# Attention stages in groups of two: three transposed banks per group, one of them copied out by ScalarE

## The reference

```
def nsa_mixer(h, ...):                      # 16 heads of 64, 4 groups of keys and values
    q, kc, vc, ks, vs, kw, vw, gates = split(h @ w_in)
    k_cmp, v_cmp = compress(kc), compress(vc)        # gelu(blocks @ w1 + b1) @ w2, 15 blocks
    p_c = masked_softmax(q k_cmp * scale + bias)     # compressed branch
    o_cmp = p_c @ v_cmp
    o_sel = softmax(q ks * scale + bias) @ vs        # 256 tokens: all 4 blocks are selected
    o_win = softmax(q kw * scale + bias) @ vw        # the window covers all 256 tokens
    g = sigmoid(gates)
    return (g[0] * o_cmp + g[1] * o_sel + g[2] * o_win) @ w_out

def fox_mixer(h, w_in, b_f, w_out):
    q, k, v, f = split(h @ w_in)
    cum = cumsum(log_sigmoid(f + b_f))
    p = masked_softmax(q k * scale + cum_i - cum_j)
    return (p @ v) @ w_out

for i in range(2):
    h = h + 0.5 * norm(swiglu(norm(h)))
    h = h + norm(mixer_i(norm(h)))
    h = h + 0.5 * norm(swiglu(norm(h)))
```

## Time and profile before

| | |
|---|---|
| time before, median of 3 runs | 1019.35 us (1019.15 to 1019.61) |
| the profiled execution, its own time | 1017.23 us |
| its span in the trace | 1015.4 us |
| TensorE busy in the span | 1003.4 us (99%) |
| VectorE / ScalarE / GpSimd busy | 637.9 / 518.0 / 118.8 us |
| NSA, 237 to 338 us of the span, FoX, 742 to 823 us | the two stretches that the change touches |

### The profile page before, as it was taken

The page is one execution under the profiler, slowest core; times in us unless marked ns, Lnnn a source line. Parts: engine busy times, 40 slices in busy tenths (PEclk is TensorE's granted clock), DMA queues, the critical chain, the costliest instruction groups (busy, mean ns, idle before and its releaser), DMA issues.

```text
span 1015.4 us, 13811 instructions
## 1 busy us (share of the span) xinstructions
PE 1003.4 (99%) x5701; PEld 849.7 (84%) x5701; DVE 637.9 (63%) x761; ACT 518.0 (51%) x711; POOL 118.8 (12%) x214
## 2 busy tenths in 40 slices
PE   8999999999999999999999999999999999999997
PEld 7888888897767898888889888888888789888886
DVE  5656555756686765555576655557568776555654
ACT  5544544644564555444465444445456665454442
POOL 1000000213263300000030000001103320000000
PEclk9999999999999999999999999999999999999999
DMA  9767779268303365566825565692485345655651
GB/s 269 257 199 259 234 258 299 86 187 248 126 2 126 125 207 186 188 201 213 291 83 194 182 205 177 196 316 98 139 281 179 108 145 176 197 195 179 206 175 74
DMA packets 138422, 189.55 MB, mean 187 GB/s; under 512 B 7442, under 2 KB 120439, under 8 KB 138360
## 3 DMA queue, kind: packets, MB, share of 16 engines
q1 hardware_dynamic: 133734, 172.83, 52.6%
q0 software_dynamic: 4480, 15.77, 4.7%
q10 hardware_dynamic: 146, 0.07, 0.0%
HBM read 185.99 MB, written 1.09 MB: 184 GB/s over the span
## 4 chain that ended last, share of the span: by engine, by line
PE 96%; DVE 1%; DMA 1%; ACT 1%; POOL 0%; issue 0%; DVEq 0%; POOLq 0%; ACTq 0%
PE ps L1203 93%; PE ps L1629 2%; PE ps L1435 1%; DMA kvN<-kvN 1%; DMA res<-in_x 0%; DVE work L957 0%; DVE late L976 0%; POOL work L468 0%; ACT work L666 0%; PE ps L1507 0%; ACT L736 0%; ACT work L583 0%; ACT normed L721 0%; DVE normed L957 0%; PE ps L1753 0%
## 5 line engine op out<-in xcount | busy, mean ns | idle before, releaser
L802 DVE TENSOR_TENSOR wlo<-raw,whi 128x2048 fp32r<-128x2048 f32 x140 | 321.1, 2294 | 122.0 <-ACT whi L551 122.0
L1203 PE MATMUL ps<-xhl,whi 128*128 128x512 f32 (+1 forms) x1664 | 370.5, 374 | 0.0
L1203 PEld LDWEIGHTS ps<-xhl,whi 128*128 128x128 f32 x1664 | 293.2, 189 | 55.2 <-issue 2.4
L551 ACT ACTIVATE whi<-raw 128x2048 fp32r<-128x2048 f32 x145 | 276.7, 1908 | 29.9 <-DMA raw<-in_fox_w_in 8.8
L1203 PEld LDWEIGHTS ps<-xhl,wlo 128*128 128x128 f32 x1536 | 196.1, 191 | 6.9 <-issue 0.4
L1203 PE MATMUL ps<-xhl,wlo 128*128 128x256 f32 x1536 | 199.8, 283 | 0.0
L1203 PE MATMUL ps<-whi,hhi 128*128 128x512 f32 x320 | 124.9, 390 | 0.0
L1203 PE MATMUL ps<-wlo,hhi 128*128 128x512 f32 x320 | 124.9, 390 | 0.0
L1203 PE MATMUL ps<-whi,hlo 128*128 128x512 f32 x320 | 124.5, 389 | 0.0
L1203 PE MATMUL ps<-whi,xhl 128*128 128x512 f32 (+1 forms) x464 | 114.6, 373 | 0.2 <-ACT xhl L591 0.2
L1203 PEld LDWEIGHTS ps<-whi,xhl 128*128 128x128 f32 x464 | 80.9, 189 | 16.8 <-issue 2.9
(11 more groups left out here) (176 smaller groups left out, 808.2 us busy)
## 6 DMA issues: line engine op xcount, KB each, us to landing
raw<-in_ffn_w_down SPq DMA_DIRECT2D x44, 1024.0 KB, 5.0
raw<-in_ffn_w_up SPq DMA_DIRECT2D x40, 1024.0 KB, 5.3
raw<-in_ffn_w_gate SPq DMA_DIRECT2D x37, 1024.0 KB, 5.3
raw<-in_fox_w_in SPq DMA_DIRECT2D x9, 1024.0 KB, 5.4
raw<-in_nsa_w_in SPq DMA_DIRECT2D x7, 1024.0 KB, 5.5
big<-in_nsa_cmp_w POOLq DMA_DIRECT2D x8, 512.0 KB, 6.8
raw<-in_nsa_w_out SPq DMA_DIRECT2D x4, 1024.0 KB, 5.2
raw<-in_fox_w_out SPq DMA_DIRECT2D x4, 1024.0 KB, 4.9
```

Of the source, the lines that this page charges most:

```text
L551: nc.scalar.activation(whi[:, u % RING, :], raw_of(u), ACT.Copy).then_inc(w_hi, 1)
L802: nc.vector.tensor_tensor(wlo[:, u % RING, :], raw_of(u), whi[:, u % RING, :].bitcast(F32), ALU.subtract).then_inc(w_lo, 1)
L1203: return nc.tensor.matmul(out_, l, r, start=start, stop=stop)
```

## The change

It sets the stages in groups of two and moves steps of the opening. On TensorE a group `g` is now `turn(g)` (12 transposes, four in each of banks GB, GB+1, GB+2; the middle bank holds the end of the first stage and the start of the second), then two `scores`, then two `heads` (with the compressed head ahead of the first in NSA). `turned_out` on VectorE copies the first and third bank (128x512 each), `middle_out` on ScalarE the second. Both heads of a group stand in one bank (HB), and `group_hi` and `group_lo` split them once per group: 128x256 in NSA, 128x512 in FoX. In `turn`, the first bank waits for the first stage's probabilities, the second and third for the second stage's; each bank waits for its copy of the group before. A probability buffer is free for the next `logits` when its transposes are done.

NSA's opening is written anew: scores of stage 0, projection 9 with the scores of stage 1 and the first compressed transposes (`compressed_T(0)`) in its middle, `compress_hidden(1)` with the second compressed scores in its middle, and stages 2 and 3 before the first turn. The compressed exponentials come ahead of the values' gelu on ScalarE instead of behind it. On VectorE the copy of `kcmp` at k == 7 comes ahead of the low part of the next weights. `hidR` moves from `late` to `flat`, and GpSimd clears it after `scale_probs(1)`. In FoX four stages (before: three) are scored inside the last three projections.

```diff
+            def middle_out(g):
+                act.wait_ge(probT_mm, 3 * g + 2)
+                if g:
+                    act.wait_ge(heads_mm, 2 * g)
+                nc.scalar.activation(probT_buf[:, 512:1024], ps[:, GB + 1, :], ACT.Copy).then_inc(middle_ready, 1)
...
+                for i in range(4, N):
+                    if i > 4 and i % 2 == 1:
+                        group_hi(i // 2 - 2)
+                        middle_out(n0 // 2 + i // 2 - 1)
+                    exps(kind, n0 + i)
+                hi(out_unit)
+                group_hi(N // 2 - 2)
+                middle_out(n0 // 2 + N // 2 - 1)
+                hi(out_unit + 1)
+                group_hi(N // 2 - 1)
...
                         evacuate(8)
+                        compressed_exp(0)
+                        exps(kind, 0)
                         hi(u0 + 11)
+                        evacuate(9)
+                        exps(kind, 1)
+                        scores_out(1)
                         part_out(1)
                         gelu(1)
-                        compressed_exp(0)
-                    evacuate(nproj - 1)
-                    attend(kind, u0 + nproj + 2, {3: lambda: scores_out(1), 6: lambda: compressed_exp(1)} if kind == "nsa" else {})
+                        exps(kind, 2)
+                        middle_out(0)
+                        exps(kind, 3)
+                        compressed_exp(1)
...
-                    nc.vector.tensor_copy(probT[:, b], ps[:, GB:GB + 2, 0:SCORES]).then_inc(probT_ready, 1)
...
+                def turned_out(g, b):
+                    dve.wait_ge(probT_mm, 3 * g + b + 1)
+                    if g:
+                        dve.wait_ge(heads_mm, 2 * g)
+                    nc.vector.tensor_copy(probT_buf[:, 512 * b:512 * b + 512], ps[:, GB + b, :]).then_inc(probT_ready, 1)
...
+                for j in range(2, G_ + 2):
+                    g = n0 // 2 + j - 2
+                    if j in before_turned:
+                        before_turned[j]()
+                    turned_out(g, 0)
+                    if j <= G_:
+                        factors(kind, n0 + 2 * j - 2)
+                    if j >= 3:
+                        group_lo(j - 3)
+                    turned_out(g, 2)
+                    if j in after_turned:
+                        after_turned[j]()
+                    if j <= G_:
+                        factors(kind, n0 + 2 * j - 1)
+                    for i in (2 * j, 2 * j + 1):
+                        if j < G_:
+                            logits(kind, n0 + i)
...
+                def turn(g, ready={}):
+                    for b in range(3):
+                        pe.wait_ge(prob_ready, 2 * g + min(b, 1) + 1)
+                        if g and b == 1:
+                            pe.wait_ge(middle_ready, g)
+                        elif g:
+                            pe.wait_ge(probT_ready, 2 * g - 1 + b // 2)
+                        if b in ready:
+                            ready[b]()
+                        for c in range(4 * b, 4 * b + 4):
+                            a, k = c // 3, c % 3
+                            last = nc.tensor.transpose(ps[:, GB + b, (c % 4) * P:(c % 4 + 1) * P],
+                                                       prob[(2 * g + a // 2) % PB][:, a % 2, k * P:(k + 1) * P], ident)
+                        last.then_inc(probT_mm, 1)
...
+                opening(scores)
+                G_ = N // 2
+                for j in range(2, G_ + 2):
+                    turn(n0 // 2 + j - 2, free.get(j, {}))
+                    if j in after_turn:
+                        after_turn[j]()
+                    if j < G_:
+                        for i in (2 * j, 2 * j + 1):
+                            scores(n0 + i)
+                    elif j == G_:
+                        pe.wait_ge(logits_ready, n0 + N)
+                        out_rows(0, 0)
+                    else:
+                        out_opening(0)
+                    for i in (2 * j - 4, 2 * j - 3):
+                        heads(n0 + i)
...
+                    def opening(scores):
+                        def second_stage():
+                            scores(1)
+                            compressed_T(0)
+                        def second_keys():
+                            pe.wait_ge(proj_ready, pr0 + 10)
+                            pe.wait_ge(probcT_ready, 1)
+                            compressed_scores(1)
+                        scores(0)
+                        project(9, second_stage)
+                        compress_hidden(1, second_keys)
+                        scores(2)
+                        compress_fold(1)
+                        turn_scores(1)
+                        scores(3)
```

More of the change, by code:

```diff
@@ L965, in factors, with attend @@
                 nc.vector.reciprocal(fac[:, b], ssum[:, b]).then_inc(fac_ready, 1)
-            def attend(kind, out_unit, after_logits):
+            def attend(kind, out_unit, after_logits={}, before_turned={}, after_turned={}):
                 n0, p0, N = STAGE0[kind], PAIR0[kind], STAGES[kind]
                 per = 2 if kind == "nsa" else 1
[L971 to L975, removed]
-                    nc.vector.tensor_copy(probT[:, b], ps[:, GB:GB + 2, 0:SCORES]).then_inc(probT_ready, 1)
[L978 to L991, removed]
-                        lo(out_unit)
[L993 to L1000, removed]
@@ L1002, in _ @@
+                lo(out_unit + 1)
+                group_lo(G_ - 1)
             nc.vector.memset(ones_row[:, :], 1.0).then_inc(ones_set, 1)
@@ L1131, in _ @@
                                 factors(kind, H + k - 10)
+                            if k == 11:
+                                logits(kind, H + 3)
                         if kind == "nsa" and k == 4:
                             gather(0)
+                        if kind == "nsa" and k == 7:
+                            dve.wait_ge(cmp_mm, 1)
+                            dve.wait_ge(kcmp_zero, 1)
+                            for r in range(2):
+                                half_ = slice(64 * r, 64 * r + 64)
+                                last = nc.vector.tensor_copy(kcmp[half_, :, r, 0:NC], ps[half_, CMB[0], 384:384 + G * NC].rearrange("p (g c) -> p g c", g=G))
+                            last.then_inc(cmp_ready, 1)
                         if k > 1:
@@ L1544, in gates, with compress_hidden @@
                 last.then_inc(gates_mm, 1)
-            def compress_hidden(kv):
+            def compress_hidden(kv, between=None):
                 pe.wait_ge(flat_ready, kv + 1)
@@ L1554, in compress_hidden @@
                 for k in range(16):
+                    if between and k == 8:
+                        between()
                     half_ = slice(64 * (k % 2), 64 * (k % 2) + 64)
@@ L1722, in compressed_scores @@
                             c0 = 32 * (pair - 4 * r)
-                            last = mm(ps[c0:c0 + 32, MB if r else YB + 2, 0:S], kcmp[:, 2 * pair // G, :, :].rearrange("p a c -> p (a c)"),
+                            last = mm(ps[c0:c0 + 32, OB if r else YB + 2, 0:S], kcmp[:, 2 * pair // G, :, :].rearrange("p a c -> p (a c)"),
                                       qT[:, pair, :], True, True)
@@ L1779, in _, with opening @@
                             gates(YB, 48, GWC)
-                    attend(kind, {}, {}, {}, out_rows, out_opening, (proj_ready, pr0 + nproj), project, nproj)
+                    def opening(scores):
+                        for i in range(4):
+                            scores(H + i)
+                            if i != 2:
+                                project(9 + (i + 1) // 2)
+                    attend(kind, opening, {}, {}, out_rows, out_opening,
+                           {2: {b: lambda b=b: pe.wait_ge(proj_ready, pr0 + nproj - 1 + b // 2) for b in (0, 2)}})
                 close_sublayer(u0 + nproj + 1, [heads_of(k) for k in range(1, 4)],
```

191 lines of the change are left out of this document (84 added, 107 removed).

## The result

The changed kernel took 1013.86 us (median of 4 runs, 1013.12 to 1016.08) against 1019.25 before on the same chip: a ratio of 0.995, 95% interval 0.9933 to 0.9968. Run once more on another chip it took 1013.19 against 1019.5, ratio 0.9947 (0.9934 to 0.996); one of the nine executions of the kernel before took 5331 us there and is left out of that ratio. The profiled execution took 1013.89 with a span of 1012.1.

A forecast was written before the change was run, and what follows sets the result against it. TensorE, busy 1003.4 of 1015.4 us, was taken as the bound. Terms -5.6 - 3.4 + 4.75 = -4.25 took the median 1019.35 to 1015.0 us (chance 0.65); own bounds 1013.3 to 1017.3, range 1011.9 to 1017.8.

The forecast's parts named there:

- the ring: Mid-NSA loop of second exponentials, factors, next logits, first exponentials, split, middle copy: 5.75 us a group, costing 2.4 of waits.
- joints: Banks now waiting on two semaphores instead of one, and other small transitions: 0.6 us of new waits (0.3 to 1.0).
- clearing of `hidR`: In NSA's opening, GpSimd's clearing, mostly covered by the first turn: 0.2 us of new waits (0 to 1.1).
- Changes of shape, -5.6: On TensorE in both mixers, 34 fewer switches of the matmul array's shape at 0.165 us each: 5.6 us saved.
- Rival B: The 0.165 us belongs to semaphores on TensorE, not array shape, so that gain vanishes: 1020.7 us, same; chance 0.09.
- Waits removed, -3.4: TensorE's waits in the two mixers that the change reaches, mostly for VectorE's copies of transposed probabilities, go: 3.4 us saved.
- FoX's two waits: In FoX, 0.75 us at the first turn for the last projection's evacuation, and 0.8 for late second-stage probabilities.
- Table loads at nothing: Two more ScalarE table loads in NSA's opening, 1.28 us each, lie beside TensorE's work and cost nothing; 2.6 if uncovered.
- Rival D: Table switches hold ScalarE about twice 1.28 us, delaying stages 2 and 3 in NSA's opening: 1017.7 us; chance 0.06.
- Rival C: GpSimd's scaling slows from 1.94 to about 3.4 us and sets the group pace at 6.8: 1021.4 us, slower; chance 0.06.
- rival A: VectorE and ScalarE run far enough ahead that waits of 2.4 and 0.8 us vanish: 1011.9 us; chance 0.14.
- mid-NSA would be no faster: Sign of being right: turns 5.6 to 5.8 us apart in mid-NSA, with the gain in openings and ends.

## Why the prediction was right, and where it was not

The forecast was 4.25 us on the trace; the two stretches gave 4.5. That it came so close is in part luck: the ring's waits were put 0.8 too low, and 0.8 was put aside for joints and the clearing of `hidR` that did not appear. The terms:

- **Changes of shape, -5.6.** Right. A group without waits takes 5.00 us (5.01 forecast), 0.17 less for each of three changes, and changes put back by hand cost 0.18 each (0.165 forecast from the gaps in the earlier trace rows). Rival B, that the price belongs to the semaphores, is refuted by the same runs, in which each group keeps its semaphores and only the order changes.
- **Waits removed, -3.4.** Right. None of the earlier trace rows is in the list after. For the `kcmp` copy the undone order shows it alone: 0.7, where 0.6 was read.
- **The ring.** Its length was right to the hundredth, 5.75, and its parts: 0.37 more on ScalarE made 0.37 more of ring, and without the middle copy it was 5.26. Its waits in NSA were sized too low. I gave the ring a head start of 0.9, by half of a stage's exponentials. From the blocks after, a turn lasts 2.20 at 284.83 instead of 1.46; the five turns lose 0.74, 0.75, 0.70, 0.31 and 0.75 by the same reading, 3.2 where I had 2.4, near the upper end of my bounds. That is about what the ring costs with no head start at all (3.7 - 0.4 = 3.3). In the third of the five, 0.24 is a wait for VectorE's copy of the compressed probabilities, for which I had no term. The 0.6 that I put aside for joints did not appear in the turns: twelve transposes with three pairs of waits take 1.46, in one turn 1.56.
- **FoX's two waits.** Recorded are 0.63 for the evacuation, and 0.73 at the third turn (0.75 and 0.8 forecast); from start to start these turns lose some 0.8 and 0.9. The timeline of TensorE:

```profile
784.42 0.63 PE L1681 MATMUL ps<-cst,work 128*128 128x128 f32 x4 [0.63 <-DVE big L1143]
...
793.75 1.09 PE L1681 MATMUL ps<-cst,work 128*128 128x128 f32 x8 [0.73 <-POOL work L470]
```

- **Table loads at nothing: the step that failed.** The cover that I named, TensorE's projection and first turn, hides them from TensorE but not from the ring, which starts on ScalarE behind them. They cost 0.5, which is no cost beside that of the ring but part of it: 0.4 of what the third turn loses and the 0.1 of the second. Rival D, with 2.6 or more, is out.
- **Clearing of `hidR`, 0.2.** The first turn is followed by `compress_out` with no wait in the list. The clearing takes 0.95 on GpSimd (at 271.59), not the 2.6 that I had from the scaling's rate.
- **Rival C.** GpSimd's scalings keep their 1.94, and in mid-NSA it waits 0.3 to 1.5 ahead of each for VectorE's factors; it does not set the pace.
- **What stood under rival A.** I said that it decides at a ring under 5.01. That was too strict. With one copy moved to VectorE the ring is 5.26, longer than TensorE's 5.00, and yet binds little in five groups. What decides is the ring's excess times the number of groups, against the lead.

That mid-NSA would be no faster was right: a group is slower, 5.74 for 5.51. Of NSA's 3.1 us, 2.0 are gained up to the transposes of stage 4, 0.1 from there to those of stage 12, and 1.0 behind them.

## What to carry to other kernels

An engine with half of its time free can still set the pace, when its instructions and another engine's wait for each other in a circle; add up the circle from starts to starts, and compare it with what the bound engine needs, group by group, since a lead can hide a small excess for a while. An instruction moved to "the idle engine" is free only outside such a circle: here 0.49 of copy a group on a ScalarE that is busy 52% made NSA 2.8 us longer than 0.60 on a VectorE that is busy 62%. And an experiment that changes nothing may only have been hidden by a wait: read it where there is no wait, or repeat it with the wait gone, as the two runs with scores and heads in turn show.

## What the runs showed of the hardware

What comes before NSA is the same work in all these kernels, yet NSA began between 237.5 and 240.1 us in their traces. It is decided in the first microseconds. The timeline of TensorE before, and after:

```profile
10.65 1.60 PE L1203 MATMUL ps<-whi,xhl 128*128 128x256 f32 x12
12.08 0.64 PE L1203 MATMUL ps<-wlo,xhl 128*128 128x256 f32 x4
```

```profile
11.27 2.19 PE L1250 MATMUL ps<-whi,xhl 128*128 128x256 f32 x12
13.30 0.64 PE L1250 MATMUL ps<-wlo,xhl 128*128 128x256 f32 x4
```

The same twelve matmuls take 12.08 - 10.65 = 1.43 and 13.30 - 11.27 = 2.03, with no wait recorded and a granted clock of 1.00 in both stretches. In narrower windows the matmuls of 256 columns start 0.21 apart at first and 0.12 apart later; the step comes at 10.0 us before and at 12.6 after. What decides when it comes was not tried and stays open; it is why lengths of stretches, which agree to 0.1 us in the two pairs of traces of one kernel, were compared here, and not spans.
